# First feed-forward: every input group with its weights stationary, and the mean square from a product of ones with squares of x

## The reference

```python
def _rms_norm(x, gain):
    xf = x.astype(jnp.float32)
    y = xf * lax.rsqrt(jnp.mean(xf * xf, axis=-1, keepdims=True) + RMS_EPS)
    return (y * gain.astype(jnp.float32)).astype(x.dtype)

def _swiglu(x, w_in, w_out):
    g, u = jnp.split(x @ w_in, 2, axis=-1)
    return (jax.nn.silu(g) * u) @ w_out

        h = _swiglu(_rms_norm(x, ffn1_pre_norm[l]), ffn1_w_in[l], ffn1_w_out[l])
        x = x + 0.5 * _rms_norm(h, ffn1_post_norm[l])
```

## Time and profile before

| | us |
|---|---|
| median of 3 runs | 889.66 (889.21 to 890.19) |
| the profiled execution's own time | 888.69 |
| its span | 887.0 |
| PE busy | 879.6 |
| DVE busy | 625.0 |
| ACT busy | 489.4 |
| POOL busy | 64.4 |

### The profile page before, as it was taken

One profiled execution on the slowest core, in us unless ns is written; L12 is line 12 of the kernel. 1 busy time (PEld: TensorE's weight loads), 2 busy tenths in 40 slices (PEclk: granted clock), 3 DMA queues, 4 the chain that ended last, 5 costly groups with the idle time before them and its releaser, 6 DMA issues.

```text
span 887.0 us, 11473 instructions
## 1 busy us (share of the span) xinstructions
PE 879.6 (99%) x4628; PEld 752.3 (85%) x4628; DVE 625.0 (70%) x808; ACT 489.4 (55%) x661; POOL 64.4 (7%) x89
## 2 busy tenths in 40 slices
PE   9999999999999999999999999999999999999997
PEld 7888888888888888888888888888999888888886
DVE  6887776467767656577577777446979857888872
ACT  6865564445444556446565555435887644555551
POOL 2000000003021110000000000000390000000000
PEclk9999999999999999999999999999999999999999
DMA  9955555455753444455655555546534456555521
GB/s 352 368 188 191 191 189 199 147 190 179 282 198 127 180 168 173 184 190 190 237 190 190 191 190 190 189 182 251 184 106 181 151 187 254 190 190 191 190 95 48
DMA packets 26948, 169.89 MB, mean 192 GB/s; under 512 B 3616, under 2 KB 3664, under 8 KB 7952
## 3 DMA queue, kind: packets, MB, share of 16 engines
q1 hardware_dynamic: 24368, 161.23, 50.3%
q0 software_dynamic: 2240, 7.66, 2.5%
q10 hardware_dynamic: 288, 0.27, 0.1%
HBM read 167.05 MB, written 1.05 MB: 190 GB/s over the span
## 4 chain that ended last, share of the span: by engine, by line
PE 97%; DVE 1%; ACT 1%; issue 0%; ACTq 0%
PE acc L1839 15%; PE acc L1642 15%; PE acc L1640 15%; PE acc L1641 15%; PE acc L2101 8%; PE acc L1841 7%; PE acc L2103 4%; PE acc L1655 2%; PE acc L1883 2%; PE acc L2053 2%; PE acc L2054 2%; PE acc L2052 2%; PE aux L2037 1%; PE aux L1764 1%; PE acc L1885 1%; PE aux L1641 1%
## 5 line engine op out<-in xcount | busy, mean ns | idle before, releaser
L996 DVE TENSOR_TENSOR w_lo<-raw,w_hi 128x2048 fp32r<-128x2048 f32 x147 | 336.8, 2300 | 89.9 <-ACT w_hi L522 89.5
L522 ACT ACTIVATE w_hi<-raw 128x2048 fp32r<-128x2048 f32 x145 | 275.7, 1911 | 62.6 <-DMA raw<-weights 62.4
L1839 PE MATMUL acc<-xT,w_hi 128*128 128x512 f32 x576 | 200.4, 394 | 0.0
L1841 PE MATMUL acc<-xT,w_lo 128*128 128x256 f32 x576 | 159.7, 277 | 0.0
L1839 PEld LDWEIGHTS acc<-xT,w_hi 128*128 128x128 f32 x576 | 108.0, 188 | 25.0
L1640 PE MATMUL acc<-w_hi,xT 128*128 128x512 f32 x312 | 124.0, 398 | 0.0
L1642 PE MATMUL acc<-w_hi,xT 128*128 128x512 f32 x312 | 121.8, 390 | 0.0
L1641 PE MATMUL acc<-w_lo,xT 128*128 128x512 f32 x312 | 121.5, 390 | 0.0
L2101 PE MATMUL acc<-xT,w_hi 128*128 128x512 f32 x320 | 111.3, 394 | 0.0
L1841 PEld LDWEIGHTS acc<-xT,w_lo 128*128 128x128 f32 x576 | 108.2, 188 | 0.0
L2103 PE MATMUL acc<-xT,w_lo 128*128 128x256 f32 x320 | 88.7, 277 | 0.0
(11 more groups left out here) (263 smaller groups left out, 1290.4 us busy)
## 6 DMA issues: line engine op xcount, KB each, us to landing
raw<-weights SPq DMA_DIRECT2D x147, 1024.0 KB, 4.8
gain_pre<-gains POOLq DMA_DIRECT2D x5, 512.0 KB, 5.0
raw<-weights SPq DMA_DIRECT2D x4, 512.0 KB, 7.5
gain_post<-gains POOLq DMA_DIRECT2D x3, 512.0 KB, 5.6
gate_w<-gate_w_in POOLq DMA_DIRECT2D x1, 1536.0 KB, 8.5
x_turned<-x_turned_in SPq DMA_DIRECT2D x4, 256.0 KB, 4.9
x<-x_in SPq DMA_DIRECT2D x2, 512.0 KB, 11.6
bias_raw<-bias_in POOLq DMA_DIRECT2D x16, 64.0 KB, 3.2
```

What stands on the lines that cost most here:

```text
L522: a.activation(w_hi[:, g % RING], raw[:, g % RING], ACT.Copy).then_inc(hi_done, 1)
L996: v.tensor_tensor(w_lo[:, slot], raw[:, slot], w_hi[:, slot].bitcast(F32), ALU.subtract)\
L1839: m.matmul(dst, w_hi[:, slot, w], xT[:, k].rearrange("p a q -> p (a q)"), start=k == 0, stop=False)
L1841: i = m.matmul(dst[:, 0:S], w_lo[:, slot, w], xT[:, k, 0], start=False, stop=k == KD - 1)
```

## The change

In the first feed-forward `STRAIGHT` becomes 0 and all 22 groups are chunks. The second feed-forward keeps four straight groups. The stream holds the first four groups in the chunks' layout.

- Loads: x turned and group 0 by alternate quarters, groups 1 and 2 by halves, groups 3 to 5, and only then x. GpSimd loads `logit` before the other constants, with a semaphore of its own.
- PE: two products of zeros of 512 columns open the two banks of chunk 0. Its first quarter has x's high part, x's low part and `w_lo` apart, as each comes; the other quarters and the halves of chunks 1 and 2 have the long products, then the short ones. In the middle of chunk 2 stands a product of ones with `sums0`. Before chunk 5 the row is turned to `rstd0` by two products of one column. The products with `rstd0_diag` and the two sets of hidden transposes are gone.
- Mean square: ACT squares `x_turned` in one instruction of 2048 elements, DVE adds the eight pieces in three steps to `sums0`, PE's product with ones gives the sum over partitions in each row. ACT's Sqrt and DVE's reciprocal then work on 256 elements, and the result is `rstd0_row` at once.
- ACT and DVE: the read-outs of chunks 0 and 1 are written out between the other work. Their gate halves are summed early and scaled when the row is there. The loop begins with pass 2, with ACT's `round_to(g0 + n + 4)` and DVE's `low_to(g0 + n + 4)`. `rates()` is cut in four: its beginning after group 3's subtraction, the rest in passes 5, 7 and 9.

The diff, cut to its core:

```diff
+STRAIGHT = {"f1_in": 0, "f2_in": 4}
+CHUNKS = {name: FF // P - n for name, n in STRAIGHT.items()}
+CHUNKS_BEFORE = {"f1_in": 0, "f2_in": CHUNKS["f1_in"]}
...
 
-        warm = at("warm", [P, P + 256], F32, area + 63488)
-        rstd0_diag = at("rstd0_diag", [P, T, P], F32, area + 65536)
+        zeros = at("zeros", [P, UNIT], F32, area + 63488)
+        ones = at("ones", [P, P], F32, area + 59392)
+        sums0 = at("sums0", [P, S], F32, area + 65536)
         rstd0_row = at("rstd0_row", [P, S], F32, area + 66560)
...
-            sp.dma_start(raw[:, 0, 2 * UNIT:].rearrange("p (j n) -> p j n", j=2),
-                         first_in[2:4].rearrange("j p n -> p j n")).then_inc(landed[0], 16)
-            for j in range(2, KD // 2):
+            for j in range(KD // 2):
                 load_turned(j)
+                sp.dma_start(raw[:, 0, j * UNIT:(j + 1) * UNIT], first_in[j])\
+                    .then_inc(landed[0] if j == 3 else unit_landed[j], 16)
...
-            sp.dma_start(raw[:, 3, :], weights[2]).then_inc(landed[3], 16)
+            for g in range(3, RING):
+                sp.dma_start(raw[:, g, :], weights[g - 1]).then_inc(landed[g], 16)
             for t in range(T):
-                sp.dma_start(x[:, t], x_in[t * P:(t + 1) * P, :]).then_inc(x_landed[t], 16)
-            for g in range(4, RING):
-                sp.dma_start(raw[:, g, :], weights[g - 1]).then_inc(landed[g], 16)
+                sp.dma_start(x[:, t], x_in[t * P:(t + 1) * P, :]).then_inc(x_landed, 16)
...
             pool.wait_ge(landed[3], 16)
+            pool.dma_start(logit[:, 0:2 * RH], decay_in.partition_broadcast(P)).then_inc(logit_in, 16)
+            pool.dma_start(logit[:, 2 * RH:], lam_in).then_inc(logit_in, 16)
             for dst, src in ((colmask, colmask_in), (conv_a, conv_a_in), (conv_ab, conv_ab_in),
                              (conv_b, conv_b_in), (gate_b, gate_b_in), (rot, rot_in)):
                 pool.dma_start(dst[:], src).then_inc(consts_in, 16)
-            pool.dma_start(logit[:, 0:2 * RH], decay_in.partition_broadcast(P)).then_inc(consts_in, 16)
-            pool.dma_start(logit[:, 2 * RH:], lam_in).then_inc(consts_in, 16)
...
-                x_hi(3)
+                for j in range(1, 4):
+                    x_hi(j)
+                    round_unit(j)
                 round_half(1, 0)
                 round_half(1, 1)
-                round_half(2, 0)
-                round_half(2, 1)
-                split[0] = 3
...
+                if which == "f1":
+                    gate_second_part(0)
+                    up_second_part(0)
+                    round_half(2, 0)
+                    round_half(2, 1)
+                    a.activation(x_squares[:].rearrange("p k q -> p (k q)"), x_turned[:].rearrange("p j e q -> p (j e q)"),
+                                 ACT.Square).then_inc(squares_ready, 1)
+                    split[0] = 3
+                    round_to(4)
+                    gate_second_part(1)
+                    up_second_part(1)
+                    act.wait_ge(sums0_full, 1)
+                    a.activation(std0_row[:], aux[:, 2, 0:S], ACT.Sqrt, bias=eps1[:], scale=1.0 / DM).then_inc(pre_std, T)
+                    act.wait_ge(ls_neg, 1)
+                    a.activation(ls[1][:], ls[0][:], ACT.Exp).then_inc(ls_exp, 1)
+                    round_to(5)
+                    for n in range(2):
+                        chunk_silu(n)
+                        chunk_round(n)
                 else:
...
+                for n in range(0 if straight else 2, chunks):
                     gate_second_part(n)
-                    round_to(g0 + 8 + n)
+                    round_to(g0 + straight + n + 4)
                     chunk_silu(n)
                     up_second_part(n)
-                    if n == 0:
+                    if straight and n == 0:
                         hidden_hi(1, 1)
                     chunk_round(n)
...
+                for j in range(4):
+                    x_lo(j)
+                    low_unit(j)
+                split[0] = 1
                 low_half(1, 0)
                 low_half(1, 1)
-                low_half(2, 0)
-                low_half(2, 1)
-                low_to(4)
...
+
+            v.memset(zeros[:], 0.0).then_inc(zeros_set, 1)
+            v.memset(ones[:], 1.0).then_inc(dve_ones_set, 1)
...
+            def rates_begin():
+
+                dve.wait_ge(logit_in, 16 * 2)
                 step(v.tensor_scalar(ls[2][:], logit[:], -1.0, None, ALU.mult))
                 v.tensor_tensor(ls[0][:], logit[:], ls[2][:], ALU.min).then_inc(ls_neg, 1)
+
...
-                c_before = CHUNKS_BEFORE[st]
+                c_before, straight, chunks = CHUNKS_BEFORE[st], STRAIGHT[st], CHUNKS[st]
+
+                def gate_sum(n):
+
+                    dve.wait_ge(gate_part, c_before + n + 1)
+                    return v.tensor_tensor(gate_c[:, n % 2], acc[:, n % 2, 0, 0:S], gate_c[:, n % 2], ALU.add)
+
+                def gate_scale(n):
+
+                    v.tensor_tensor(gate_c[:, n % 2], gate_c[:, n % 2], rstd0_row[:], ALU.mult).then_inc(gate_summed, 1)
 
                 def chunk_gate(n):
 
-                    b = n % 2
-                    dve.wait_ge(gate_part, c_before + n + 1)
                     if which == "f1":
-                        if n == 0:
-                            dve.wait_ge(rstd0_row_ready, 1)
-                        step(v.tensor_tensor(gate_c[:, b], acc[:, b, 0, 0:S], gate_c[:, b], ALU.add))
-                        v.tensor_tensor(gate_c[:, b], gate_c[:, b], rstd0_row[:], ALU.mult).then_inc(gate_summed, 1)
+                        step(gate_sum(n))
+                        gate_scale(n)
                     else:
...
+                if which == "f1":
+                    step(gate_sum(0))
+                    chunk_up(0)
+                    low_half(2, 0)
+                    low_half(2, 1)
+                    dve.wait_ge(squares_ready, 1)
+                    step(v.tensor_tensor(x_squares[:, 0:4], x_squares[:, 0:4], x_squares[:, 4:8], ALU.add))
+                    step(v.tensor_tensor(x_squares[:, 0:2], x_squares[:, 0:2], x_squares[:, 2:4], ALU.add))
+                    v.tensor_tensor(sums0[:], x_squares[:, 0], x_squares[:, 1], ALU.add).then_inc(sums0_ready, 1)
+                    step(gate_sum(1))
+                    chunk_up(1)
+                    low_to(4)
+                    rates_begin()
+                    dve.wait_ge(pre_std, T)
+                    v.reciprocal(rstd0_row[:], std0_row[:]).then_inc(rstd0_row_ready, 1)
+                    dve.wait_ge(rstd0_row_ready, 1)
+                    gate_scale(0)
+                    gate_scale(1)
+                    chunk_product(0)
+                    chunk_low(0)
+                    low_to(5)
+                    chunk_product(1)
+                    chunk_low(1)
                 else:
...
+                for n in range(0 if straight else 2, chunks):
                     chunk_gate(n)
-                    low_to(g0 + 7 + n)
+                    low_to(g0 + n + (7 if straight else 4))
                     chunk_up(n)
-                    if n == 0:
+                    if straight and n == 0:
                         hidden_lo(1, 1)
+                    if not straight and n == 5:
+                        rates_ratio()
+                    if not straight and n == 7:
+                        rates_series()
+                    if not straight and n == 9:
+                        rates_end()
                     chunk_product(n)
                     chunk_low(n)
+                    if not straight and n == 4:
+                        dve.wait_ge(rstd0_turned, 1)
+                        v.tensor_copy(rstd0[:], aux[:, 3, 0:T]).then_inc(rstd0_ready, 1)
...
+                def long_products(c, ks):
+                    for half in range(2):
+                        for k in ks:
+                            m.matmul(acc[:, c % 2, half], weight(c, w_hi, k, half), xT[:, k].rearrange("p a q -> p (a q)"),
+                                     start=k == 0, stop=False)
+
+                def short_products(c, ks):
+                    for half in range(2):
+                        for k in ks:
+                            i = m.matmul(acc[:, c % 2, half, 0:S], weight(c, w_lo, k, half), xT_hi[:, k],
+                                         start=False, stop=k == KD - 1)
+                        if ks[-1] == KD - 1:
+                            i.then_inc(chunk_full if half else gate_chunk_full, 1)
+
+                pe.wait_ge(zeros_set, 1)
+                for half in range(2):
+                    m.matmul(acc[:, 0, half], zeros[:, 0:P], zeros[:], start=True, stop=False)
+                pe.wait_ge(unit_hi, 1)
+                pe.wait_ge(first_hi, 1)
+                for half in range(2):
+                    for k in range(2):
+                        m.matmul(acc[:, 0, half, 0:S], weight(0, w_hi, k, half), xT_hi[:, k], start=False, stop=False)
```

(91 more changed lines are left out.)

214 lines of the change are left out of this document (66 added, 148 removed).

## The result

| kernel | median us | lowest to highest | runs |
|---|---|---|---|
| before | 890.19 | 889.21 to 890.58 | 5 |
| changed | 903.80 | 903.30 to 904.22 | 5 |

The ratio is 1.016, with the interval 1.0149 to 1.0171. The prediction was 904.2, between 899.5 and 908.0, slower with a chance of 0.90. The profiled execution of the changed kernel took 903.80, its span 902.1; before it was 888.69 and 887.0.

What follows compares the result with a forecast made beforehand. PE (99% busy) bounds the kernel, and late ACT and DVE read-outs open waits: an 8.2 us stall at chunk 4, 0.17 per chunk and 3.4 for rates delay the second tile 14.5, giving 904.2 against the 889.66 median; range 899.5 to 908.

Steps and rivals of the forecast that it cites:

- The opening: First chunks on PE: chunk 0 done at 11.7 to 12.1, PE ready for chunk 4 at about 29, no gain.
- PE's own work -0.24: PE's added and removed instructions net -0.24 us, bounds -0.44 to 0; hidden inside PE's waits, so counted for nothing.
- The chain to chunk 2's up sum: Logits, exp, rounding, silu, products and subtractions on ACT and DVE delay this sum to 37.2; PE stands 8.2 us.
- The drain at a table load: Rival at silu's table load: ACT empty another 1.4 us before silu, giving 905.6; chance 0.02.
- The passes: DVE waits for each pass's rounding in the chunk loop: cycle 5.73 us, up from 4.78, against PE's 5.56 a chunk.
- The rates: Rate pieces in passes 5, 7 and 9 are no longer hidden and add 3.4 us.
- The end: Chunk 21's up_summed at 37.2 + 19 x 5.73 + 3.4 = 149.5 starts the output stage's second token tile, +14.5.
- Slow after the pause: Rival: PE at half rate after its rest before chunk 4 loses 2.7 us; 907 if rates don't swallow it; chance 0.08.
- The loop at PE's pace: Rival: loop passes take 5.56 us, the chunk 4 stall and rates remain; +11.1, or 901; chance 0.12.
- late logits: Rival: logit lands at 26.4, as in its old place, instead of 23.9; +2.5, or 906.7; chance 0.10.
- The read-outs in time: Rival: chunk 4 finds its banks free, leaving PE's -0.24 and the opening's gain; 889.4, not slower; chance 0.10.
- What would show it: Trace signs: PE idle about 8 us before chunk 4, waits of 0.2 per chunk, 1.2 to 1.5 before 8, 10, 12.

Runs made afterwards that it cites:

- e7: e6 with the two small products that turn rstd0 placed before chunk 4 instead of chunk 5; 890.40 us, ratio 1.0008 to the kernel before.
- e1: Changed kernel with DVE subtracting one group later in each first feed-forward pass (low_to with n + 3, not n + 4); 898.93 us, ratio 1.0103 to before.
- e4: Kernel before, with DVE subtracting in the first feed-forward's loop the group that ACT rounds in the same pass; 894.52 us, ratio 1.0058 to before.
- e2: Changed kernel with the three later pieces of the rates moved from passes 5, 7 and 9 to behind the loop; 900.77 us, ratio 1.0129 to before.
- e6: Changed kernel with four gate/up buffers, subtraction one group behind, rates and exp moved away, group 4 rounded before the square root; 891.63 us, ratio 1.0022 to before.
- e3: Changed kernel with ACT rounding group 4 ahead of the square root instead of behind exp; 902.84 us, ratio 1.0149 to before.
- e5: e6 with DVE subtracting the group that ACT rounds in the same pass, and low_to(7) in pass 3; 895.82 us, ratio 1.0068 to before.
- e9: Changed kernel with GpSimd's loads of logits and lambdas issued after the second weight group landed, not the fourth; 902.82 us in one run.
- e8: e6 with four more, useless 128-column PE products behind the small ones ahead of chunk 5; 891.55 us, ratio 1.0017 to before.

## Why the prediction was right, step by step

- *The number.* The mechanism is right; that 904.2 comes within 0.4 of 903.80 is in part luck. The sum was +14.5. The output stage's second tile moved by 14.8, the profiled execution by 15.1, the median by 13.6 (890.19 to 903.80; the forecast had started from 889.66). Within the sum, terms missed both ways: +0.14 at the first up sum, 19 x 0.015 = 0.28 too much for the passes, 0.07 too much for the rates, 0.42 that stood in none.
- *What bounds.* The one semaphore followed, `up_summed`, is the one that PE waits for: 8.6 us in all, and 7.3 of it before chunk 4.
- *The opening.* Optimistic by 1. Chunk 0 ended at 12.7, not 11.7 to 12.1; x's second part landed at 6.6 and held up ACT for 1.58. With three chunks of 5.65 to 5.77 and the sum product PE was ready at 30.2, not 29.0. It cost nothing, as PE would have stood anyway: the pause was 7.3 in place of 8.2 and ended where it was to end. That e7 starts its output stage 0.21 before the old kernel agrees with "PE's own work -0.24", but executions differ by more than that.
- *The chain to chunk 2's up sum.* Right: forecast to end at 37.2, measured 36.92 + 0.42 = 37.34. Logits: DVE starts on them at 24.01 (23.9), exp 24.49 (24.3), rounding 24.62 (24.5), table 26.54 (26.4), silu 27.84 (27.7), low part of chunk 0 29.20, subtraction 29.54 (29.4), group 5's rounding 32.78 (32.7), its subtraction 34.71 (34.6). DVE came there at 23.69, not 23.0, because ACT had rounded group 2's second half at 16.45, not 15.7; the logits hid that, with 0.32 to spare. The reciprocal took 1.74, the value that was chosen between 0.42 and 3.6.
- *The drain at a table load.* Silu starts 1.30 after its load starts, 1.28 of that the load. The rule of the Trainium skill, "ScalarE: Activation LUTs", section "What ACT_TABLE_LOAD costs", that 1.38 us of drain come on top, isn't borne out here, and the sum was right to leave it out.
- *The passes.* 5.715 in place of 5.73, and e1 and e4 show the mechanism from both sides: take the index back and the passes are 4.78 until PE sets the pace, put it into the old kernel and they are 5.72.
- *The rates.* Passes 5, 7 and 9 take 6.68, 7.01 and 6.78, together 3.33 over three of 5.715, against 3.4. e2 moves them away and takes 3.35 out of DVE's loop.
- *The end.* 37.34 + 19 x 5.715 + 3.33 + 0.42 = 149.68, and PE starts there at 149.79; forecast 149.5. The 0.42 is the one term that was in no sum.
- *The rivals.* Slow after the pause did happen, and in the changed kernel it cost nothing. PE by stretch in the changed kernel (columns as above):
```profile
29.00:37.00 8.00, 1.21 (x8) 0.79 (x6) 6.43 (x8) 3.54 (x7) 0.00 (x0) 0.88 1.02 414
37.00:41.00 4.00, 3.51 (x11) 3.06 (x12) 2.53 (x7) 3.07 (x5) 0.00 (x0) 0.50 0.37 153
41.00:45.00 4.00, 4.00 (x22) 3.46 (x21) 3.38 (x6) 1.39 (x3) 0.00 (x0) 0.89 0.00 0
45.00:60.00 15.00, 15.00 (x88) 13.05 (x87) 10.76 (x20) 7.83 (x13) 0.00 (x0) 1.00 0.53 180
```
PE had stood idle for 7.28 us. From 37 to 41 the granted clock is 0.50, the lower of its two levels (1.2 of 2.4 GHz), and a pair of a long and a short product takes 0.64 in place of 0.35; from 42 on the clock is full again. Chunk 4 took 8.0 in place of 5.65, so PE lost some 2.4 us and came behind DVE's loop. It then ran without a wait until the passes with rates let it catch up. The first weight loads that wait for another engine again:
```profile
74.43 0.19 PEld L1861 LDWEIGHTS acc<-xT,w_hi 128*128 128x128 f32 x1 [0.75 <-DVE w_lo L985]
...
86.93 0.19 PEld L1861 LDWEIGHTS acc<-xT,w_hi 128*128 128x128 f32 x1 [1.19 <-DVE w_lo L985]
```
So the slow clock was hidden behind what the rates cost DVE, and where e2 takes the rates away it shows: there PE, not DVE, sets the start of the second token tile. This agrees with the rule of the Trainium skill, "TensorE: Matmul & The Clock Gate", section "Part 1: The HAM clock gate", that an idle array falls back to half of its rate until work has released it, which the trace of before could not show after a pause. *The loop at PE's pace* and *late logits* did not occur. *The read-outs in time*, the rival on the other side, was no property of this kernel, but e6 and e7 built it: e7's median is 890.4 where that rival had said 889.4.
- *What would show it.* Of the waits foretold for PE only the first came as described. Those of 1.2 to 1.5 before chunks 8, 10 and 12 were 0 (still behind, as above), 0.75 and 1.19. Those of 0.2 before each chunk are there only from 74.47 on, shorter, and too short for PE's list, which names three waits: chunks then start 5.70 to 5.73 apart (but for the pass with rates), and their pairs fill 5.55 in six of twelve and 5.65 in the other six (last section), which leaves 0.16 or 0.06. From 45.50 to 68.19 PE was behind and ran at 5.65 without a wait. The signs on DVE and ACT all came. The time depends on DVE alone there, so it didn't suffer.

## What to carry to other kernels

Where two engines hand a stream to each other, compare the index that each one names in the same pass: ahead by one is hidden, the same index puts a whole hand-over (here 0.95 us a pass) into the cycle, and no total of the page shows it. When a stage's opening is rebuilt, write out the in-order list of the engine that frees the buffers: what was cheap under cover (rates, subtractions of later groups) stands ahead of a read-out that now is urgent. Delay ahead of a loop that is bound by its slowest member stays whole to the end (e3), and what is taken out of that member counts only until the next one is the bound (e2).

## What the runs showed of the hardware that was not expected

- **Two paces of the same pairs.** A product of 512 columns and one of 256, each with its own weight load, take together 0.3467 us in some stretches and 0.3533 in others, at a granted clock of 1.00 in both and with no wait: 5.55 or 5.65 a chunk. A stretch keeps its pace until something else, or a wait, comes between the pairs: in the changed kernel, where PE waits a little before each chunk from 74.47 on, the pace changes from chunk to chunk. Before, the changed kernel, e2, e3, e5, e6, e7 and e9 ran the second feed-forward's chunks from the second on at 0.3467, e1, e4 and e8 at 0.3533, in their profiled executions. That is 17 x 16 x 0.0067 = 1.8 us, and the profiled executions of e1 (899.34) and e4 (896.01) stand 1.9 and 1.7 over what was expected of them. In the first feed-forward, before (from its second chunk on), e7 and e1 had the quick pace behind the turn or the transposes, and e2, e6 and e8 the slow one. What picks it is open: not the presence of an interruption (e8 has a longer one), and one trace for each kernel can't say whether the place decides or chance. Two kernels that differ by less than 0.2% here may differ by nothing else.
- **0.42 us in one pass.** The product in pass 4 starts 0.94 after the up sum in place of 0.52, and the profile names nothing but that sum itself to wait for. It is there in the changed kernel, e2, e3 and e9 alike, at the same place in the program. In e5 and e6, whose code is laid out otherwise, pass 4 does not have it. Nor does it in e1, which differs from the changed kernel by one index. Not explained.
- **A reciprocal is dear by the element:** 0.160 us for 1 column, 0.278 for 20, 1.74 for 256, that is 6.2 ns each, where an addition of 256 takes 0.42.
